# Four modulation matrices in one stage, streamed through TensorE in column quarters

## What is computed

```python
cs = jax.nn.silu(c)
for l in range(DEPTH):                                  # DEPTH = 2
    mod = cs @ ada_w[l] + ada_b[l]                      # 1024 x 6144, twice
...
    # in shared_kv: cs @ kv_ada_w + kv_ada_b            # 1024 x 2048
...
mod_x = (silu(c_2) @ w_mod_2[0] + b_mod_2[0])           # 1024 x 6144
mod_c = (silu(c_ctx_2) @ w_mod_2[0] + b_mod_2[0])       # the same matrix, a second vector
```

## Time and profile before

| | us |
|---|---|
| median of 3 runs | 6293.67 |
| lowest and highest run | 6289.52, 6301.94 |
| span of the profiled execution | 6278.8 |
| from the first issue of `ada_w` to the last VectorE instruction of the fourth matrix | 12.95 to 319.22 |

### The profile page before, as it was taken

The page is one execution under the profiler, slowest core; times in us unless marked ns, Lnnn a source line. Parts: engine busy times, 40 slices in busy tenths (PEclk is TensorE's granted clock), DMA queues, the critical chain, the costliest instruction groups (busy, mean ns, idle before and its releaser), DMA issues. The chain is left out here.

```text
span 6278.8 us, 52914 instructions
## 1 busy us (share of the span) xinstructions
PE 5120.2 (82%) x20330; PEld 2500.9 (40%) x20330; DVE 1663.1 (26%) x3413; ACT 891.7 (14%) x1549; POOL 0.2 (0%) x4
## 2 busy tenths in 40 slices
PE   2587377776999997889879999965894678599998
PEld 2532366643333332334433333343443633333332
DVE  7812633422111111013221111113007610211111
ACT  0001111112111112122121111122102210200001
POOL 0000000000000000000000000000000000000000
PEclk9998788987999998875679999977897789799999
DMA  8620000003666650100046666521120021087774
GB/s 322 228 80 15 4 0 0 0 27 136 240 240 240 236 192 28 54 28 0 27 155 233 232 237 240 187 69 35 43 67 1 1 80 49 9 318 274 277 275 150
DMA packets 396549, 790.14 MB, mean 126 GB/s; under 512 B 19408, under 2 KB 104528, under 8 KB 396448
## 3 DMA queue, kind: packets, MB, share of 16 engines
q1 hardware_dynamic: 396448, 788.81, 35.3%
HBM read 786.68 MB, written 2.10 MB: 126 GB/s over the span
## 5 line engine op out<-in xcount | busy, mean ns | idle before, releaser
L1333 PE MATMUL ps<-arena 128*64 128x512 f32 x3072 | 1248.9, 594 | 4.3 <-ACT arena L1373 4.3
L335 PE MATMUL ps<-arena 128*128 128x512 f32 (+1 forms) x2560 | 1074.7, 583 | 184.0 <-DMA arena<-in_w_in 51.5
L335 PEld LDWEIGHTS ps<-arena 128*128 128x128 f32 x2560 | 501.1, 197 | 755.5 <-issue 566.6
L1333 PEld LDWEIGHTS ps<-arena 128*64 128x64 f32 x3072 | 398.7, 137 | 786.6 <-issue 786.6
L1362 PE MATMUL ps<-arena 128*64 128x512 f32 x1536 | 589.6, 595 | 6.2 <-ACT arena L1373 6.2
L1438 DVE TENSOR_TENSOR arena<-arena,ps 128x512 f32<-128x512 f32 x48 | 33.0, 687 | 1170.0 <-ACT arena L1389 1170.0
L1314 PE MATMUL ps<-arena 128*128 128x512 f32 x688 | 334.3, 618 | 7.2 <-ACT arena L1373 3.5
L1304 PE MATMUL ps<-arena 128*128 128x512 f32 x688 | 311.0, 606 | 30.7 <-DVE small L1426 30.7
L1362 PEld LDWEIGHTS ps<-arena 128*64 128x64 f32 x1536 | 188.4, 137 | 368.5 <-issue 368.5
L1373 ACT ACTIVATE arena<-ps 128x512 f32<-128x512 f32 x340 | 180.7, 599 | 1080.3 <-PE ps L1304 559.5
L1414 DVE TENSOR_SCALAR arena<-arena,small 128x64 f32<-128x64 f32 x344 | 59.9, 250 | 794.7 <-PE ps L1362 758.6
(11 more groups left out here) (337 smaller groups left out, 4693.2 us busy)
## 6 DMA issues: line engine op xcount, KB each, us to landing
arena<-in_moe_wgate SPq DMA_DIRECT2D x64, 2048.0 KB, 9.6
arena<-in_moe_wup SPq DMA_DIRECT2D x64, 2048.0 KB, 14.4
arena<-in_moe_wdown SPq DMA_DIRECT2D x64, 2048.0 KB, 8.4
arena<-in_w_e_gate SPq DMA_DIRECT2D x32, 2048.0 KB, 7.9
arena<-in_w_e_up SPq DMA_DIRECT2D x32, 2048.0 KB, 12.8
arena<-in_w_e_down SPq DMA_DIRECT2D x32, 2048.0 KB, 8.7
arena<-in_ada_w SPq DMA_DIRECT2D x24, 2048.0 KB, 12.3
arena<-in_w_in SPq DMA_DIRECT2D x36, 1024.0 KB, 7.7
```

The costliest lines, as they stand in the source:

```text
L335: mm = nc.tensor.matmul(K.ps[:, b * 4 + m, 0:tok], wb[b][:, k, m * P:(m + 1) * P], rhs[:, k, :], start=(k == 0), stop=(k == kt - 1))
L1333: last = mm(K.ps[half[b], j, :], xg[:, k, half[b]], W[b][j][:, k, :], start=(k == 0), stop=(k == KT - 1))
```

## The change

All four matrices are handled in one stage, `modulations`, that replaces the four calls.

- **Layout.** Feature `p * 8 + k` now lies on partition `p` (the host arranges `c`, `c_2` and `c_ctx_2` so). A partition's eight matrix rows are then neighbours in HBM. A piece is 128 partitions x 6144 numbers: for the three wide matrices one `k` of all columns, a run of 24 KB for each partition; for `kv_ada_w` three `k` (the last piece two). There are 8 + 8 + 3 + 8 = 27 pieces instead of 40 chunks, in four buffers of 3 MB each, and SyncE goes from one matrix to the next without a stage's end between them.
- **Product.** VectorE has no part in it. TensorE holds the vector as stationary operand, 128 x 32, of which one column (two for `w_mod_2`) is the vector and the rest zero (`cpad`), and the matrix is the moving operand, 512 columns at a time. Column block `n` goes to the column quarter `n % 4` of the array and so to PSUM partitions 32 (n % 4) and up, in bank `n // 4`. Each piece is 12 such matmuls; all of them accumulate over `k` in PSUM (three banks for each of two matrices in turn).
- **Turning.** When a matrix is complete, ScalarE copies its three banks to SBUF (`rows`), TensorE turns them with 12 small matmuls against columns of the identity matrix (4 for `kv_ada_w`), and VectorE adds the bias and the ones. For all but the last matrix this stands behind the first piece of the next matrix.
- **SiLU** moves from `setup` into the new stage: VectorE clears `cpad`, ScalarE writes the three vectors into it, TensorE waits for that.

```diff
-def modulation(K, W, ncols, first, nv, bias, dst, ones_at):
...
+def modulations(K):
...
+    wb = [K.arena[:, 6:12, :].rearrange("p a b -> p (a b)")[:, b * WIDE:(b + 1) * WIDE] for b in range(B)]
+    cpad = K.flat(8, 2 * KT * 32).rearrange("p (g k v) -> p g k v", g=2, k=KT)
+    rows = [K.flat(16 + 4 * j, 3 * 512).rearrange("p (b n) -> p b n", b=3) for j in range(2)]
...
+            for m, (j, a, deep) in enumerate(pieces):
+                W, ncols = jobs[j][:2]
+                if m >= B:
+                    sp.wait_ge(used, m - B + 1)
+                sp.dma_start(wb[m % B][:, 0:deep * ncols].rearrange("p (k n) -> p k n", k=deep),
+                             W.rearrange("(p k) n -> p k n", k=KT)[:, a:a + deep, :]).then_inc(w_in[m % B], 16)
...
+            def turn(j):
+                W, ncols, group, nv = jobs[j][:4]
+                pe.wait_ge(lifted, j + 1)
+                if j >= 2:
+                    pe.wait_ge(biased, j - 1)
+                pick = K.ident[:, :].rearrange("p (q w) -> p q w", w=32)[:, :, 0:nv]
+                for b in range(ncols // 2048):
+                    for m in range(4):
+                        mm = nc.tensor.matmul(K.ps[:, 6 + j % 2, (b * 4 + m) * 4 * nv:(b * 4 + m + 1) * 4 * nv].rearrange("p (q v) -> p q v", v=nv),
+                                              rows[j % 2][:, b, m * P:(m + 1) * P], pick, start=True, stop=True)
+                mm.then_inc(turned, 1)
+
+            pe.wait_ge(padded, 3)
+            for m, (j, a, deep) in enumerate(pieces):
+                W, ncols, group, nv = jobs[j][:4]
+                pe.wait_ge(w_in[m % B], (m // B) * 16 + 16)
+                if a == 0 and j >= 2:
+                    pe.wait_ge(lifted, j - 1)
+                for k in range(deep):
+                    for n in range(ncols // 512):
+                        q = slice(32 * (n % 4), 32 * (n % 4) + 32)
+                        mm = nc.tensor.matmul(K.ps[q, 3 * (j % 2) + n // 4, :], cpad[:, group, a + k, :],
+                                              wb[m % B][:, k * ncols + n * 512:k * ncols + (n + 1) * 512],
+                                              start=(a + k == 0), stop=(a + k == KT - 1))
+                mm.then_inc(used, 1)
+                if j and m == last_piece[j - 1] + 1:
+                    turn(j - 1)
+            turn(len(jobs) - 1)
...
+            for j in range(len(jobs)):
+                act.wait_ge(used, last_piece[j] + 1)
+                if j >= 2:
+                    act.wait_ge(turned, j - 1)
+                nb = jobs[j][1] // 2048
+                nc.scalar.activation(rows[j % 2][:, 0:nb, :], K.ps[:, 3 * (j % 2):3 * (j % 2) + nb, :], ACT.Copy).then_inc(lifted, 1)
...
+    def rows(a):
+        return np.asarray(a).reshape(P, -1)
...
-        "c": flat(inputs["c"]), "c_2": flat(inputs["c_2"]), "c_ctx_2": flat(inputs["c_ctx_2"]),
+        "c": rows(inputs["c"]), "c_2": rows(inputs["c_2"]), "c_ctx_2": rows(inputs["c_ctx_2"]),
```

More of the change, by code:

```diff
@@ L188, in setup @@
     with Stage(nc) as S:
-        loaded, own_d, own_a = S.sem("loaded"), S.sem("own_d"), S.sem("own_a")
+        loaded, own_d = S.sem("loaded"), S.sem("own_d")
         block = S.block()
@@ L206, in _ @@
             o.seal(nc.vector.tensor_scalar(K.vs("qnorm8"), K.vs("qnorm"), HD ** -0.5, None, ALU.mult))
[L208 to L213, removed]
-def modulation(K, W, ncols, first, nv, bias, dst, ones_at):
+def modulations(K):
     nc = K.nc
-    W = W.rearrange("(k p) n -> p k n", p=P)
+    ins = K.ins
+    jobs = [(ins["ada_w"][l], 6 * D, 0, 1, K.vs("ada_b")[:, 48 * l:48 * l + 48], K.mod[l], (8, 16, 32, 40)) for l in range(DEPTH)]
+    jobs += [(ins["kv_ada_w"], 2 * D, 0, 1, K.vs("kv_ada_b"), K.modkv, (8,)),
+             (ins["w_mod_2"][0], 6 * D, 1, 2, K.vs("b_mod"), K.mod2, (8, 32))]
     B = 4
[L225 to L229, removed]
+    WIDE = 6 * D
+    wb = [K.arena[:, 6:12, :].rearrange("p a b -> p (a b)")[:, b * WIDE:(b + 1) * WIDE] for b in range(B)]
+    cpad = K.flat(8, 2 * KT * 32).rearrange("p (g k v) -> p g k v", g=2, k=KT)
+    rows = [K.flat(16 + 4 * j, 3 * 512).rearrange("p (b n) -> p b n", b=3) for j in range(2)]
+    pieces = []
+    for j, (W, ncols, group, nv, bias, dst, ones_at) in enumerate(jobs):
+        deep = WIDE // ncols
+        pieces += [(j, a, min(deep, KT - a)) for a in range(0, KT, deep)]
+    last_piece = [max(m for m, piece in enumerate(pieces) if piece[0] == j) for j in range(len(jobs))]
     with Stage(nc) as S:
-        w_in, rounds, own = S.sems("w_in", B), S.sem("pe_rounds"), S.sem("own")
-        pe_s = Steps(S.sem("pe_steps"), [f"chunk{b}" for b in range(B)], lead=1)
-        dve_s = Steps(S.sem("dve_steps"), [f"b{b}k{k}v{v}" for b in range(B) for k in range(KD) for v in range(nv)], lead=1)
+        w_in = S.sems("w_in", B)
+        blank, padded, used, lifted, turned, biased, own = (S.sem(x) for x in (
+            "blank", "padded", "piece_used", "rows_lifted", "turned", "biased", "own"))
         block = S.block()
@@ L245, in _ @@
         @block.tensor
         def _(pe):
[L247 to L253, removed]
-                    for m in range(4):
[L255 to L263, removed]
@@ new lines, in _ @@
+            turn(len(jobs) - 1)
+        @block.scalar
+        def _(act):
+            act.wait_ge(blank, 1)
+            for n, name in enumerate(("c", "c_2", "c_ctx_2")):
+                nc.scalar.activation(cpad[:, (n + 1) // 2, :, n // 2], K.vs(name), ACT.Silu).then_inc(padded, 1)
+            for j in range(len(jobs)):
[4 more added lines that the diff above has]
+                nc.scalar.activation(rows[j % 2][:, 0:nb, :], K.ps[:, 3 * (j % 2):3 * (j % 2) + nb, :], ACT.Copy).then_inc(lifted, 1)
@@ L266, in _ @@
         @block.vector
         def _(dve):
[L268 to L282, removed]
@@ L283, in _ @@
-            loop(dve, n // B, body)
-            o = Own(dve, own)
[L285 to L292, removed]
+            o = Own(dve, own)
@@ new lines, in _ @@
+            nc.vector.memset(cpad, 0.0).then_inc(blank, 1)
+            for j, (W, ncols, group, nv, bias, dst, ones_at) in enumerate(jobs):
+                n = ncols // P
+                dve.wait_ge(turned, j + 1)
+                sums = K.ps[:, 6 + j % 2, 0:n * nv].rearrange("p (b m q v) -> p b m q v", m=4, q=4, v=nv)
+                for v in range(nv):
+                    to = dst[:, :] if nv == 1 else dst[:, :, v]
+                    o.mark(nc.vector.tensor_tensor(to.rearrange("p (b q m) -> p b q m", q=4, m=4), sums[:, :, :, :, v].rearrange("p b m q -> p b q m"),
+                                                   bias.rearrange("p (b q m) -> p b q m", q=4, m=4), ALU.add))
+                o.join()
+                dve.sem_inc(biased, 1)
+                for at in ones_at:
+                    d = dst[:, at:at + KT] if nv == 1 else dst[:, at:at + KT, :]
+                    o.mark(nc.vector.tensor_scalar(d, d, 1.0, None, ALU.add))
+                o.join()
@@ L1704, in first_block @@
     ins = K.ins
[L1705 to L1708, removed]
+    modulations(K)
     X = K.slot(S_X)
```

2 lines of the change are left out of this document (removed).

## The result

| | before | changed |
|---|---|---|
| median, us | 6291.6 (4 runs) | 6189.95 (4 runs) |
| lowest to highest, us | 6280.65 to 6301.94 | 6188.09 to 6196.62 |
| span of the profiled execution, us | 6278.8 | 6188.6 |
| next stage (`scale_shift`) begins, us | 319.72 | 222.55 |

The ratio is 0.9839 with a 95% interval of 0.9824 to 0.9855, so 1.6% faster; 6199 us were forecast, in a range of 6186 to 6232. A second measurement of the same two kernels, both on one chip, gave 6287.55 and 6193.19, ratio 0.9848 (0.9835 to 0.9861), so the saving is 94 to 102 us.

A forecast was written before the change was run, and what follows sets the result against it. VectorE's pace and the joints were taken to bound the old stage (306.3 us), the load the new one: 2.7 + 199.8 + 9.1 = 211.6 us, 94.7 less, so 6293.7 - 94.7 = 6199 us, range 6186 to 6232.

The forecast's parts named there:

- What bounded the stage: In the modulation stages before, VectorE paces each matrix (5.91 or 7.43 us a chunk), with 8.9 us joints; 306.3 us in all.
- The load: Loading 83.9 MB of matrices unbroken at 420 GB/s takes 199.8 us (191 to 217), plus 2.7 us latency at both ends.
- The straight line through the earlier trace: Time per DMA packet, fitted through the 2 KB and 4 KB stretches, gives 439 GB/s for 24 KB packets.
- The rival of colliding runs: In the load, runs 192 KB apart collide in HBM; at half of 387 GB/s the kernel takes 6433 us; chance 0.05.
- The start: At the stage's start, VectorE's clearing and ScalarE's SiLUs end before the first piece lands at 23 us and cost nothing.
- The tail: Behind the last piece: matmuls 3.2 us, copy 1.8, turning 2.9, VectorE 0.8, four hand-overs at about 0.1; together 9.1 us.
- TensorE beside the load: In the new stage, a piece's 12 matmuls mostly fit under its 7.5 us arrival, so TensorE costs nothing beside the load.
- That rival: TensorE becomes the stage's bound: blocks run serially and the clock stays at 1.2 GHz; kernel 6283 us; chance 0.04.
- Clock: TensorE stands at 1.2 GHz in the old modulation stages despite printed 1.00; lagging without gaps, it would rise to 2.4 GHz.
- SyncE waiting for `used`: In the new stage, SyncE waiting for buffers to be freed, with TensorE busy without gaps, would show the forecast wrong.
- Span and median: For the whole kernel, the median stands 14.9 us above the profiled span; expected span 6184 us, saving taken off the median.
- Sum: The new stage takes 2.7 + 199.8 + 9.1 = 211.6 us against 306.3, so 94.7 us less.

The follow-up runs named there:

- experiments from both sides: From before: part of the product left out of the kernel before, 6241.25 us. From after: the changed kernel with four separate stages and 2 KB runs, 6253.25 us.

## Why the prediction was right, and where it was not

- **What bounded the stage**: right. VectorE's pace and the joints were read off the timeline, and experiments from both sides return the pace (46 us from before, 40.8 from after); the joints' 40.2 us are measured from after alone.
- **The load** (2.7 + 199.8 us): taken at 420 GB/s, measured 427 over 16 to 210 us. From the first issue at 12.08 to the last piece at 210.60 it took 198.5 instead of 202.5 us. The straight line through the earlier trace rows, 439, came out nearer than the last measured row, 412. The limit of about 358 GB/s for one core that the Trainium skill gives (DMA: Bandwidth & Descriptors, Specifications), there half of a stack's 716, doesn't hold for this run, whose kernel runs on one core: 430 GB/s for 160 us. The rival of colliding runs took the runs of before for neighbours; by the layout (feature `k * 128 + p` on partition `p`) they stood 24 KB apart from partition to partition, and the run with that distance has 429 GB/s.
- **The start**: `setup` gave up its SiLUs at the end of its path, most of the 0.9 us by which the stage begins earlier; the prediction counted them as free in their new place and nothing as gained in the old.
- **The tail** (9.1 us): 11.4 measured, 210.60 to 222.04. The last piece 4.2 (3.2), the copy with its wait 1.5 (1.8), the turning 5.0 (2.9), VectorE 0.7 (0.8). The mis-sized terms are the two of TensorE, and they have one cause, the next point. The last piece was saved from 5.3 us by a clock that rose while it ran.
- **TensorE beside the load**: the step that failed. "A 128 x 512 fp32 matmul follows the last after 0.43 us" took a record for a matmul; a matmul is two records, 0.86 us at the higher clock. Twelve in a row are then 10.3 us at the *higher* clock, not at the lower. TensorE at nothing beside the load was said to need no overlap unless the clock stayed low ("only 2 us are lost"); the run with one quarter, at a granted clock of 1.00, shows that without overlap 90 us are lost even at the higher level. That rival was given 4 in 100 and a condition too many. That its 6283 us is also what one quarter measured is a coincidence: 320 times 0.855 at the lower clock is nearly 640 times 0.43 at the higher. The forecast held because the quarters do run side by side, 3.7 times; that part of its argument was right, and with it a factor of two too little for each matmul did no harm, which was luck: 5.3 us at the lower clock still fit into 7.3. The Trainium skill (TensorE: Matmul & The Clock Gate, Part 3) has 2.38 times for three column tiles, and the trace, 3.7 for four, is above it in proportion. The count was there to be made: the earlier trace rows has 416 weight loads of line 261, where the program has 28 x 4 + 12 x 4 x 2 = 208 matmuls, and the "608 short matmuls" are 304. In `linear`, 8 matmuls stand between two evictions, and in the trace of before these follow each other after 6.87 us, 16 times 0.43:

```profile
343.08 0.60 ACT L360 ACTIVATE arena<-ps 128x512 f32<-128x512 f32 x1 [20.43 <-PE ps L335]
...
349.95 0.60 ACT L360 ACTIVATE arena<-ps 128x512 f32<-128x512 f32 x1 [6.27 <-PE ps L335]
```

- **Clock**: right that a lagging TensorE gets the higher level: with one quarter, where it never catches up, the granted clock is 1.00. Right too that the printed 1.00 in the modulation stages of before was not to be trusted: the weight load takes 330 ns there, and 190 in the dense work behind.
- **A sign that doesn't tell**: SyncE waiting for `used` was named as a sign of being wrong. It waits so for 165.0 us in the changed kernel too, since four buffers are soon full; in the run with one quarter it is 243.4.
- **Span and median**: "the median stands 14.9 us above the span" mixed two things. An execution is 1.8 us above its own span (6190.35 and 6188.6); the profiled execution of before was simply the fastest, 6280.65. The saving was taken off the median, so the forecast didn't hang on it. The expected span of 6184 did: it started from a fast execution, and 6188.6 were measured.
- **Sum**: 94.7 us forecast, 97.2 at the start of the next stage: 4.0 more from the load, 0.9 from the start, 2.3 less from the tail, errors that partly cancel. In the medians 101.7 and 94.4. Of the 9 us between 6199 and 6189.95, 2.1 are the base (a fourth run brought the median of before from 6293.67 to 6291.6), 2.5 the stage, and the rest the scatter behind it.

## What to carry to other kernels

Before costing matmuls from a trace, count its records between two evictions against the program's instructions: here fp32 matmuls stand twice. A product of one vector with a matrix that the load should pace can go to TensorE with the matrix as moving operand, and there the column quarters decide whether it fits under the load: in one quarter a piece took 10.3 us against 7.3. Check how many are needed (two here); with four the granted clock was lower, and the stage only 1.3 us shorter than with two. And when a stage turns into one chain of loads, look at what breaks the chain (joints, 13 us each) and at what stands ahead of it (10.7 us here) before its rate.

## What the runs showed that was not expected

- A run of 24 KB is one packet, and the rate goes 387 or 398 GB/s (2 KB), 412 (4 KB), 430 (24 KB), with 24 or 192 KB between neighbouring partitions' runs alike. Where the 11 GB/s between the two kinds of 2 KB load come from stays open.
- Taking the quarters one after the other in program order still overlaps them, two records at a time on average (5.43 us for 24).
- The two runs with a slower order end the stage earlier than the changed kernel, at 221.94 and 220.27 against 222.55: behind a busier TensorE the tail's turning takes 2.85 us instead of 4.86. With two quarters it took 4.76, at a mean granted clock of 0.95 before it, so this can't be counted on.
- The same instructions behind the stage take 5959 to 5975 us, more than several of the effects above; a marker at the end of the changed stage resolves what the medians don't.
